# Expert sums two gathered groups at a time, their products in turn on the two column halves of TensorE

## The reference, cut to what matters

```python
def block(hb):
    ...
    top, sel = lax.top_k(cand, PEER_TOPK)
    eidx = jnp.take_along_axis(cidx, sel, axis=-1)
    g = jax.nn.softmax(top, axis=-1)
    act = jax.nn.gelu(jnp.einsum('nd,nhkd->nhk', hb, expert_u[eidx]).astype(jnp.float32), approximate=False)
    return jnp.einsum('nhk,nhkd->nd', (g * act).astype(hb.dtype), expert_v[eidx])
```

## Time and the profile before

| | |
|---|---|
| median of 3 runs | 3,954.36 us (3,952.37 to 3,976.56) |
| the profiled execution | 3,957.28 us |
| its span in the profile | 3,955.5 us |
| granted TensorE clock, mean of the span | 0.895 |
| PE, DVE, ACT, POOL busy | 78%, 62%, 39%, 31% of the span |

### The profile page before, as it was taken

The page is one execution under the profiler, slowest core; times in us unless marked ns, Lnnn a source line. Parts: engine busy times, 40 slices in busy tenths (PEclk is TensorE's granted clock), DMA queues, the critical chain, the costliest instruction groups (busy, mean ns, idle before and its releaser), DMA issues. The chain is left out here.

```text
span 3955.5 us, 44026 instructions
## 1 busy us (share of the span) xinstructions
PE 3065.7 (78%) x11624; PEld 1441.8 (36%) x11624; DVE 2461.9 (62%) x6411; ACT 1555.4 (39%) x4273; POOL 1245.4 (31%) x1139
## 2 busy tenths in 40 slices
PE   8799978557786886778688858886888688757876
PEld 2466653332252243224332423252335233411331
DVE  0222222488678668766776777677757775956695
ACT  0233321236524442553354335534552454333433
POOL 0000012023323443433333324433343334334333
PEclk9698889688998998899899979998998799979979
DMA  8211123399998999999999999999999899989998
GB/s 321 81 38 38 38 71 135 129 339 370 382 364 341 412 385 390 366 414 375 370 392 407 394 354 387 398 399 345 399 407 378 337 403 407 391 325 417 410 386 368
DMA packets 299713, 1291.64 MB, mean 327 GB/s; under 512 B 39271, under 2 KB 135415, under 8 KB 163125
## 3 DMA queue, kind: packets, MB, share of 16 engines
q0 software_dynamic: 156672, 1124.27, 70.8%
q1 hardware_dynamic: 142780, 164.51, 12.7%
HBM read 1271.34 MB, written 17.79 MB: 326 GB/s over the span
## 5 line engine op out<-in xcount | busy, mean ns | idle before, releaser
L1660 PE MATMUL YY<-ring,dg 128*64 128x512 f32 (+1 forms) x4224 | 1737.0, 659 | 590.5 <-ACT dg L1231 567.9
L1102 POOL DMA_INDIRECT ring<-experts_dram,idxc x1056 | 1196.4, 1133 | 1917.2 <-PE YY L1660 1701.1
L1505 DVE CUSTOM_DVE_ANT_0 ring<-ring,h2c 128x1024 f32<-128x1024 f32 x1056 | 1265.7, 1224 | 557.4 <-DMA ring<-experts_dram,idxc 548.6
L1660 PEld LDWEIGHTS YY<-ring,dg 128*64 128x64 f32 (+1 forms) x4224 | 517.8, 147 | 1657.8 <-ACT dg L1231 952.3
L1221 ACT ACTIVATE ga<-act 128x1 f32<-128x1 f32 x1056 | 212.5, 201 | 1028.9 <-DVE act L1505 1027.1
L1231 ACT ACTIVATE dg<-fold,gw 128x64 f32<-128x64 f32 x1024 | 356.4, 348 | 50.9 <-PE YY L1660 1.8
L1641 PE MATMUL M<-fT,wq 128*128 128x128 f32 (+1 forms) x2304 | 299.1, 293 | 74.7 <-DMA wq<-w_query_dram 74.6
L1223 ACT ACTIVATE gw<-ga,gc 128x1 f32<-128x1 f32 x1056 | 311.5, 295 | 35.2 <-ACT ga L1221 1.0
L1641 PEld LDWEIGHTS M<-fT,wq 128*128 128x128 f32 x2304 | 290.8, 209 | 79.6 <-DMA wq<-w_query_dram 78.2
L1256 DVE SCALAR_TENSOR_TENSOR yac<-win,cw,yac 128x128 f32<-128x128 f32 x960 | 262.7, 346 | 0.0
L530 PE MATMUL A<-w_in,hT 128*128 128x512 f32 (+1 forms) x432 | 210.7, 652 | 0.0
(11 more groups left out here) (305 smaller groups left out, 2561.0 us busy)
## 6 DMA issues: line engine op xcount, KB each, us to landing
wq<-w_query_dram SPq DMA_DIRECT2D x72, 1024.0 KB, 22.3
wa<-w_ada_dram SPq DMA_DIRECT2D x12, 2048.0 KB, 7.9
ring<-experts_dram,idxc POOLq DMA_INDIRECT x1056, 13.2
w_in<-w_in_dram SPq DMA_DIRECT2D x1, 10272.0 KB, 33.5
kh<-kT_scratch SPq DMA_DIRECT2D x16, 264.0 KB
xb<-x_prompt_dram SPq DMA_DIRECT2D x8, 512.0 KB, 5.2
t_xb<-x_prompt_dram SPq DMA_DIRECT2D x8, 512.0 KB, 11.2
w_o<-w_o_dram SPq DMA_DIRECT2D x8, 512.0 KB, 5.1
```

The costliest lines, as they stand in the source:

```text
L1102: pool.indirect_dma_start(ring[:, k % RING, :], None, I["experts"], bass.IndirectOffsetOnAxis(idxc[:, k:k + 1], 0)).then_inc(g_in[k % RING ...
L1505: v.tensor_tensor_reduce(out=u, in0=u, in1=h2, scale=1.0, scalar=0.0, op0=ALU.mult, op1=ALU.add, accum_out=act8[:, k % RING:k % RING + 1]) ...
L1660: mm = pe.matmul(YY[o, half * 512:(half + 1) * 512], dg[:, k % DG, 0:w], ring[:, k % RING, D + half * 512:D + (half + 1) * 512], start=(k ...
```

## The change

For prompt blocks `sums` now returns at even groups and at an odd one handles both: it waits for the odd group's diagonal (`diag_done` at NG * e + k + 1, which covers the even one), and issues the first 512 columns of the even group, those of the odd group, and then the second 512 columns of both. `v_done` is still raised once for each group, now at the ends of the two last products. The sampled rows' groups are summed one by one as before.

```diff
                 w = TS if smp else HALF
+                if not smp and k % FOLD == 0:
+                    return
+                pair = [k] if smp else [k - 1, k]
                 pe.wait_ge(diag_done, NG * e + k + 1)
-                if k == 0 and some(e):
+                if k < FOLD and some(e) and pair[0] == 0:
                     pe.wait_ge(y_ready, e)
-                o = slice(0, w) if smp else slice(k % FOLD * HALF, (k % FOLD + 1) * HALF)
                 for half in range(2):
-                    mm = pe.matmul(YY[o, half * 512:(half + 1) * 512], dg[:, k % DG, 0:w],
-                                   ring[:, k % RING, D + half * 512:D + (half + 1) * 512],
-                                   start=(k == 0 if smp else k < FOLD),
-                                   stop=(k == groups_of(e) - 1 if smp else k >= NG - FOLD), skip_group_check=True)
-                mm.then_inc(v_done, 1)
+                    for i in pair:
+                        o = slice(0, w) if smp else slice(i % FOLD * HALF, (i % FOLD + 1) * HALF)
+                        mm = pe.matmul(YY[o, half * 512:(half + 1) * 512], dg[:, i % DG, 0:w],
+                                       ring[:, i % RING, D + half * 512:D + (half + 1) * 512],
+                                       start=(i == 0 if smp else i < FOLD),
+                                       stop=(i == groups_of(e) - 1 if smp else i >= NG - FOLD), skip_group_check=True)
+                        if half:
+                            mm.then_inc(v_done, 1)
```

## The result

| | |
|---|---|
| before | 3,958.36 us median (3,952.37 to 3,976.56, 6 runs) |
| changed | 4,001.88 us median (3,989.62 to 4,011.08, 6 runs) |
| ratio | 1.0099, 95% interval 1.007 to 1.0128 |
| the profiled execution of the changed kernel | 4,011.08 us, span 4,009.3, mean granted clock 0.816 (0.895 before) |

The changed kernel is 1.0% slower. 4,014 us was said; the direction is right, and the loss is about 40 us where 60 were worked out.

A forecast was written before the change was run, and what follows sets the result against it. Gather transfers through the eight ring slots were taken as the limit, slowed where slots return late. 3,957.3 + 48 (delay) + 12 (clock) = 4,017 us, stated as 4,014 because the profiled execution stood 2.9 above the median; range 3,962 to 4,115.

The forecast's parts named there:

- Products in turn: TensorE products alternating between column halves: worth nothing, since neighbouring groups' products already overlap, twelve matmuls in 3.65 us.
- Waiting for the partner: Even groups' ring slots come back one 2.97 us gap later; mean delay 1.5 us a gather, bounds 1.5 and 2.1.
- that sign of being wrong: Steps' own products ending so much sooner that VectorE idles less in the routing steps would refute the forecast.
- Three of the other signs: Product line busy 1,000 to 1,200 us; lower rate in fifth, ninth, tenth stretches; pair ending near 2 us after second diagonal.
- How much of the delay counts: Delay over 128 ring turns, 192 us, of which a quarter was counted: 48 us, bounds 0 and 81.
- the other three stretches: Fifth, ninth and tenth of an iteration's ten windows, 368 to 388 GB/s, neither transfers nor VectorE full; delay counts there.
- The clock: 12 us: Less busy TensorE falls to granted clock 0.80, making a pair's four steps 1.7 us longer; 12 us in all.
- Place behind step products and ScalarE's four buffers: Step products going one group earlier at some steps, and even diagonals waiting for ScalarE's buffers: both counted as nothing.
- Hidden after all: Rival: gather queue and waiting data cover the delay everywhere; price 0 to 40 us, 3,954 to 3,994; chance 0.32.
- Groups one after another: Rival: groups' products mostly run serially now, so pairs finish some 1.3 us sooner; 3,897 us; chance 0.06.
- The ring as the bound throughout: Rival: every delay of a ring slot counts; 4,146 to 4,223 us; chance 0.05.
- The clock falls further: Rival: TensorE's granted clock falls to 0.72 on average, as in the tenth stretch; about 4,120 us; chance 0.10.

The follow-up runs named there:

- experiment 1: Changed kernel with its two inner loops exchanged: waits for the odd diagonal, then all even-group products, then all odd; 4,000.09 us, ratio 1.0097 to before.
- experiment 2: Changed kernel, but each group waits only for its own diagonal, keeping the pair's place in TensorE's program; 3,959.22 us, ratio 0.9993 to before.
- experiment 6: Kernel before (with held slots): products at once, even slot given back only with the odd group's; 3,980.28 us, ratio 1.0042; changed kernel beside it 1.0086.
- experiment 4: Kernel before, each prompt group's products waiting for the next group's diagonal, except at block ends, groups still summed singly; 3,999.36 us, ratio 1.0103.
- experiment 3: Changed kernel with pairs only for groups 0 to 49 of a block: 3,970.5 us, ratio 1.0013; only for groups 50 to 127: 3,986.66 us, 1.006.
- experiment 8: Changed kernel plus one 512-column zero matmul in the gap ahead of a pair, after the even group's diagonal; 3,992.16 us, ratio 1.0073 to before.

## Why the prediction was right, point by point

- *Products in turn are worth nothing.* Shown by experiment 1, and by the pair of 1.94 us with the products in program order. The burst in the earlier trace rows had said so.
- *Waiting for the partner delays the even slot by a gap, and that is what costs.* That the wait and not the place is the cause, experiment 2 shows. The median landing went down by 1.1 us and VectorE's waits for landings up by 48 us, as named. In the iteration shown VectorE idles for 37.6 us in the last four stretches, the routing steps, where it was 32.8; that sign of being wrong did not come. Three of the other signs failed: the product line is busy for longer than said, the tenth stretch did not lose rate, and a pair at 1.2 GHz ends some 3.5 us after its second diagonal and not 2.
- *How much of the delay counts: a quarter, 48 us.* Mis-sized. It measured 17 us (experiment 6, 0.42% of 3,965), a share of 0.09 of 192 us; experiment 4 has 0.11 with twice the delay. I let no stretch with full transfers or full VectorE count, and most of the other three stretches. Two things eat more than I allowed: a landing that is 1.1 us sooner takes up most of the mean delay, and of the 49 us of added waits for landings 25 came back at the routing scores (experiment 6), a place that the term did not have. The places were about right (experiment 3: little in attention, most in the rest), though not each stretch: the first, with the largest fall in rate, I had as covered.
- *The clock: 12 us.* The clock was said to be 0.80, and the iteration has 0.83. Its price was too low: 17 us lie between experiment 6 and the changed kernel, with the same slots and diagonals held back. For 11 of them the rows at the blocks' ends show the clock: a block's last pair costs VectorE 3.07 us of waiting at 2.4 GHz and up to 4.8 at 1.2. That the other 6 are the clock's fits, and is not shown: experiment 8 brought the clock back in part and its time does not decide. The way was another than I had worked out. The term took a slower pair as a slot that is late by 1.7 us, with a share of a quarter; but VectorE waits no longer for landings than in the kernel with held slots, and waits for the last pair itself, of which I had said nothing.
- *Place behind step products and ScalarE's four buffers: nothing.* The place, yes. ScalarE now waits for the buffers 41 us in 42 places where it waited 1.8 us; I had counted nothing. Its waits for the routing products went down from 469 to 417 us. I had written that VectorE is busy meanwhile; not always: its own wait for the scores made of them went from 110.6 to 92.5 us. Whether the scores come sooner or VectorE later is not separated here; with held slots ScalarE's wait fell by 18 us alone (to 451) and VectorE's by 25. ScalarE's two rows of the waits view:

```profile
ACT qh L1182 <- PE M L1641: 417.4, 64, 13.1
...
ACT dg L1231 <- PE YY L1664: 41.4, 42, 13.5
```

- *The rivals.* Hidden after all: the delay's own 17 us lie within what this rival allowed (0 to 40), and the whole loss of 39 by the ratio is at its upper end, at the border of 1%. What it has wrong is that the rest is no delay of slots. Groups one after another: experiment 1 rules it out. The ring as the bound throughout: experiment 4 rules it out, since 380 us of delay cost 41. The clock falls further: no, its mean is 0.82 and not 0.72.

Together the two terms were 60 us, and the two timings of the changed kernel gave 34 and 39: the delay was taken too large (48 for 17) by more than the clock too small (12 for up to 17). The two errors go opposite ways, which brought the sum some 5 us nearer by luck; the range was wide enough for a delay term nearly three times too large.

## What to carry to other kernels

Before making two pieces of work run together, look in the trace whether they do so already: twelve matmuls in 3.65 us, where four alone take 1.93, say it in one row. A wait that pairs things gives buffers back later even if the pair is done faster; how much that costs is the part of the delay that is not eaten elsewhere, by a queue or by a wait that ends when it did before, here a tenth and not the quarter that the stretches suggested. And an engine that is made less busy may run slower: here PE lost 342 us of work and with it a part of its clock. Look then for the places where another engine waits for its last result: 11 us of the loss stand at eight block ends.

## What was not expected of the hardware

- Matmuls on one column half do not wait for earlier ones in the program on the other half: a pair takes 1.94 us whether its eight matmuls are ordered by group or in turn.
- Matmuls with zero weights raise the granted clock: 0.81 to 0.90 with one 512-column zero product after each group on both halves, and that kernel, with more work, became 0.8% faster.
